# Causal attention on one Trainium2 core: scores, turned probabilities and values issued two items a period

## The chip, the cores and the metric

The kernel runs on one core of one Trainium2 chip. The metric is the device time of one execution in microseconds (us); three executions were timed. A difference is judged against what three executions of this kernel can tell apart.

## The reference

Two transformer blocks over 512 tokens of width 1024. The first block is a gated delta layer and then a sparse attention layer, each with an MLP. The part that matters here is the attention layer's two causal branches, "selected" and "window". With 512 tokens, 16 blocks chosen of 8 and a window of 512, both are plain causal softmax attention over 16 heads with 64 columns each, with their own keys and values and their own gate:

```
scale = dh ** -0.5
...
p_s = masked_softmax(jnp.einsum('bqghd,bgqkd->bghqk', qr, k_sel), (kpos <= t[:, None])[:, :, None])
o_s = jnp.einsum('bghqk,bgqkd->bqghd', p_s, v_sel)
...
p_w = masked_softmax(jnp.einsum('bqghd,bkgd->bghqk', qr, kwin), m_w)
o_w = jnp.einsum('bghqk,bkgd->bqghd', p_w, vwin)
g = take(gates)
o = g[..., 0:1] * o_c + g[..., 1:2] * o_s + g[..., 2:3] * o_w
```

The second block (latent attention beside a Fourier branch, two layers) is not touched.

## The kernel before, in words

All engines run fixed programs, in order, and wait for each other by semaphores. Weights stream through a ring of three blocks: a DMA brings `raw`, ScalarE rounds it to `w_hi` (L1724), GpSimd takes the rest as `w_lo` (L3480), TensorE does three matmuls for each product (L957 to L959). PSUM has eight banks; `plan_core` gives every product a bank and a count, `claim` waits until the bank's last reader has released it, `fill` announces it and `read` waits until it has been read.

The causal stage works through 48 items, `NSA_ITEMS`: for each of 8 pairs of heads (`j`) the six steps of `NSA_STEPS`. An item is one tile of 128 queries (`qt`) with one or both of the branches, for the two heads `s` = 0 and 1. Its width for a head is 2, 4, 3, 3, 4, 4 tiles of 128 keys for the steps 0 to 5; steps 0 and 1 hold both branches. The items of this text are written by their number n and step n mod 6. Each passes through six pieces of work:

- **S(n)**, TensorE, L1444 and L1448: scores into a pair of banks, (4, 5) for even n and (0, 1) for odd n. Three passes for two heads, on tiles of 64 rows, and four or eight small bf16 matmuls that add the causal mask.
- **max(n)**, VectorE, L3130: the row maxima. Then **exp(n)**, ScalarE, L2263: two or four exponentials with row sums into `prob[n % 4]`; with the last the scores' banks are free.
- **scale(n)**, VectorE, L3137 and L3142: reciprocals of the sums, and two or four multiplications of `prob` by reciprocal and gate.
- **T(n)**, TensorE, L1459: 2w transposes (w is the width) of `prob` into banks 6 and 7, one bank for each head.
- **copy(n)**, ScalarE, L2256: the turned probabilities out of both banks into `probT[n % 4]`, in one instruction.
- **V(n)**, TensorE, L1479: 4w matmuls of 128 columns, on tiles of 64 columns, adding to the output bank 2 or 3 of the head pair. At step 0 of each head pair from j = 2 on, four matmuls of `block_values` (L1433, "BV") stand ahead of V; those of j = 0 and 1 stand behind S(1).

When a head pair has its last V, ScalarE rounds the output (`a_hi`, L2271) and VectorE takes the rest (`a_lo`, L3121). ScalarE also rounds two weight blocks in the stage.

The order before, for i = 0 to 50, is S(i), T(i-2), V(i-3) on TensorE; copy(i-2), exp(i) on ScalarE; max(i), scale(i-1) on VectorE. Steady state is one item of each kind for each i.

Of the kernel before, what the change touches and what calls it, by code (L numbers as in the profile page):

```python
# [23 lines left out]
ACT = mybir.ActivationFunctionType  # L24
ALU = mybir.AluOpType
# [31 lines left out]
NSA_STEPS = [(0, (0, 1)), (1, (0, 1)), (2, (0,)), (2, (1,)), (3, (0,)), (3, (1,))]  # L57
NSA_ITEMS = [(j, qt, brs) for j in range(8) for qt, brs in NSA_STEPS]
NSA_LAST = len(NSA_STEPS) - 1


NSA_PARTS = [("q", 0), ("q", 1), ("keys", 0), ("keys", 1), ("q", 2), ("q", 3)]
# [313 lines left out]
def plan_core():  # L376
# [18 lines left out]
    def take_pair(key, b):  # L395

        take(key, b)
        beside[key] = uses[b + 1]
# [520 lines left out]
def prob_count(n, s, b):  # L919

    full, rest = divmod(n, len(NSA_STEPS))
    widths = [2 * len(brs) for _, brs in NSA_STEPS]
    return full * sum(widths) + sum(widths[:rest]) + s * len(NSA_ITEMS[n][2]) + b + 1


def program_tensor(pe, nc, c, block, bank, split, beside, early, sum_blocks):
# [23 lines left out]
    def read(key):  # L950

        b, n, _ = bank[key]
        pe.wait_ge(c.bank_read[b], n + 1)
# [472 lines left out]
    halves_of = [slice(64 * s, 64 * s + 64) for s in range(2)]  # L1426
    outs = {}

    def block_values(j):
# [5 lines left out]
    for i in range(len(NSA_ITEMS) + 3):  # L1435
        if i < len(NSA_ITEMS):
            j, qt, brs = NSA_ITEMS[i]
            end, out, both = (qt + 1) * P, claim_pair(("s1", i)), slice(brs[0], brs[-1] + 1)
            halves = [out[:, s, 0:len(brs) * end].rearrange("p (b k) -> p b k", b=len(brs)) for s in range(2)]
            if i % len(NSA_STEPS) == 0 and j in NSA_PARTS_FROM:  # L1440
                pe.wait_ge(c.score_lo, NSA_PARTS_FROM[j])
            for n, (q, k) in enumerate(((c.q_lo1, c.keys_hi), (c.q_hi1, c.keys_lo), (c.q_hi1, c.keys_hi))):
                for s, r in enumerate(halves_of):
                    mm(halves[s], q[r, j, qt * P:end], k[r, both, j // 4, 0:end], start=n == 0, stop=False)  # L1444
            for part, first in ((0, 64), (1, 0)):
                for s, r in enumerate(halves_of):
                    at = qt * P + 64 * part
                    ins = mm(halves[s][:, :, at:at + 64], c.causal16[r, first:first + P],  # L1448
                             c.causal16[r, 192:256].unsqueeze(1).to_broadcast([64, len(brs), 64]), start=False, stop=part == 1)
            ins.then_inc(fill(("s1", i)), 1)  # L1450
        if 2 <= i < len(NSA_ITEMS) + 2:
            n = i - 2
            j, qt, brs = NSA_ITEMS[n]
            out = claim_pair(("t1", n))
            for s in range(2):
                for b in range(len(brs)):
                    pe.wait_ge(c.prob_ready, prob_count(n, s, b))
                    for kt in range(b * (qt + 1), (b + 1) * (qt + 1)):
                        ins = nc.tensor.transpose(out[:, s, kt * P:kt * P + P], c.prob[:, n % 4, s, kt * P:kt * P + P], ident)  # L1459
            ins.then_inc(fill(("t1", n)), 1)  # L1460
        if i == 1:
# [6 lines left out]
        if i >= 3:  # L1468
            n = i - 3
            j, qt, brs = NSA_ITEMS[n]  # L1470
            if j > 1 and n % len(NSA_STEPS) == 0:
                block_values(j)
            read(("t1", n))
            last = n % len(NSA_STEPS) == NSA_LAST
            for b, br in enumerate(brs):
                for kt in range(qt + 1):
                    for s, o_rows in enumerate(halves_of):
                        v0, at = br * 256 + (2 * (j // 4) + s) * 64, (b * (qt + 1) + kt) * P
                        ins = mm(outs[j][o_rows, qt * P:qt * P + P], c.v[:, kt, v0:v0 + 64], c.probT[:, n % 4, s, at:at + P],  # L1479
                                 start=False, stop=last and kt == qt)  # L1480
            if last:
                ins.then_inc(c.attn_out, 1)
# [215 lines left out]
def program_scalar(act, nc, c, block, bank, split, beside, early, n_blocks, sums, squares_behind):  # L1698
# [73 lines left out]
    def release(key):  # L1772
        return c.bank_read[bank[key][0]]
# [477 lines left out]
    for i in range(len(NSA_ITEMS) + 3):  # L2251
        if 2 <= i < len(NSA_ITEMS) + 2:
            key, (_, qt, brs) = ("t1", i - 2), NSA_ITEMS[i - 2]
            n, end = i - 2, len(brs) * (qt + 1) * P
            filled(key)
            f(c.probT[:, n % 4, :, 0:end], c.pairs[bank[key][0] // 2][:, :, 0:end], ACT.Copy).then_inc(release(key), 1)  # L2256
        if i < len(NSA_ITEMS):
            key, (_, qt, brs), end = ("s1", i), NSA_ITEMS[i], (NSA_ITEMS[i][1] + 1) * P
            act.wait_ge(c.nb_ready, i + 1)
            for s in range(2):  # L2260
                for b in range(len(brs)):
                    e, m = slice(b * end, (b + 1) * end), s * len(brs) + b
                    ins = f(c.prob[:, i % 4, s, e], c.pairs[bank[key][0] // 2][:, s, e], ACT.Exp, bias=c.nb[:, i % 4, m:m + 1],  # L2263
                            accum_out=c.nb[:, i % 4, 4 + m:5 + m])
            ins.then_inc(release(key), 1)
        if i in (5, 11):
            weights(first + 4 + i // 6)
        if i >= 4 and (i - 4) % len(NSA_STEPS) == NSA_LAST:
            j = (i - 4) // len(NSA_STEPS)
# [246 lines left out]
def program_vector(dve, nc, c, block, bank, split, early, sums):  # L2516
# [25 lines left out]
    def step(ins):  # L2542

        ins.then_inc(c.vector_step, 1)
        count["step"] += 1
        dve.wait_ge(c.vector_step, count["step"])
# [577 lines left out]
    for i in range(len(NSA_ITEMS) + 2):  # L3124
        if i < len(NSA_ITEMS):
            key, (_, qt, brs) = ("s1", i), NSA_ITEMS[i]
            n, end = len(brs), (qt + 1) * P
            filled(key)
            scores = c.pairs[bank[key][0] // 2][:, :, 0:n * end].rearrange("p s (b k) -> p s b k", b=n)
            v.reduce_max(c.nb[:, i % 4, 0:2 * n].rearrange("p (s b) -> p s b", s=2), scores, axis=AX, negate=True)\  # L3130
                .then_inc(c.nb_ready, 1)
        if 1 <= i <= len(NSA_ITEMS):
            n = i - 1
            j, qt, brs = NSA_ITEMS[n]
            read(("s1", n))
            w, end = 2 * len(brs), (qt + 1) * P
            step(v.reciprocal(c.nb[:, n % 4, 8:8 + w], c.nb[:, n % 4, 4:4 + w]))  # L3137
            for s in range(2):
                for b, br in enumerate(brs):
                    m, g = 8 + s * len(brs) + b, NSA_H * (1 + br) + 2 * j + s  # L3140
                    e = c.prob[:, n % 4, s, b * end:(b + 1) * end]
                    v.tensor_scalar(e, e, c.nb[:, n % 4, m:m + 1], c.gate[:, qt, g:g + 1], ALU.mult, ALU.mult)\  # L3142
                        .then_inc(c.prob_ready, 1)
        if i >= 5 and (i - 5) % len(NSA_STEPS) == NSA_LAST:
            out_parts((i - 5) // len(NSA_STEPS))
    out_parts(7)
    sums_before_norm(3, "out", 1)

# [403 lines left out]
```

## Time and profile before

| | |
|---|---|
| median of three executions | 2000.17 us (2000.13 to 2001.76) |
| the profiled execution | 2002.18 us, of which the span of the profile 2000.1 us |
| causal stage in the span, first S to first matmul of the output projection | 767.18 to 903.53 us, 136.35 us |
| TensorE clock granted in the stage | full (1.00) |

A line of the profile gives the source line, the engine (PE is TensorE's matmuls, PEld its weight loads, DVE VectorE, ACT ScalarE), the operation, output and inputs by the program's names, and the shape. A matmul's end is modelled, so its stated length is longer than the step to the next one's start; the starts tell how fast TensorE goes on.

### The profile page before, as it was taken

How to read it: one execution, taken by the hardware profiler on the slowest of the kernel's cores; microseconds unless marked ns; L12 is line 12 of the kernel's file. 1: busy time of each engine (PE TensorE's matmuls, PEld its weight loads, DVE VectorE, ACT ScalarE, POOL GpSimd, SP SyncE). 2: the span in 40 equal slices, each digit the busy share in tenths (PEclk: the TensorE clock that was granted, in tenths of full speed). 3: DMA queues.
4: the chain of work that ended last, by engine and by line, in shares of the span. 5: the costliest groups of instructions: out<-in, count | busy, mean ns of one | idle time of the engine just before them, and what ended most of it. 6: DMA issues, size and time to landing. Idle time of an engine off the chain costs nothing.

```text
span 2000.1 us, 31685 instructions
## 1 busy us (share of the span) xinstructions
PE 1978.2 (99%) x12682; PEld 1662.3 (83%) x12682; DVE 1272.2 (64%) x2271; ACT 1056.8 (53%) x1770; POOL 749.2 (37%) x380
## 2 busy tenths in 40 slices
PE   8999999999999999999999999999999999999999
PEld 6877788988988887778888889878789987878897
DVE  7885556566656358873665665667777734777781
ACT  7752465444436327883643443567664544767441
POOL 3442134444444641003444444344044444413543
PEclk9999999999999999999999999999999999999999
DMA  4442123333322431002233333222013322211332
GB/s 163 127 133 83 48 87 106 104 103 100 106 96 95 142 106 38 12 2 99 95 106 99 104 104 103 87 95 85 23 53 106 105 96 95 77 40 42 102 103 93
DMA packets 62465, 178.18 MB, mean 89 GB/s; under 512 B 17760, under 2 KB 18144, under 8 KB 62320
## 3 DMA queue, kind: packets, MB, share of 16 engines
q1 hardware_dynamic: 47312, 166.99, 25.4%
q10 hardware_dynamic: 15008, 9.16, 1.7%
q8 instruction: 102, 1.67, 0.3%
q14 instruction: 43, 0.35, 0.1%
HBM read 170.85 MB, written 3.70 MB: 87 GB/s over the span
## 4 chain that ended last, share of the span: by engine, by line
PE 87%; DVE 7%; ACT 4%; issue 2%; POOL 0%; DMA 0%; ACTq 0%; DVEq 0%
PE banks L957 18%; PE banks L958 18%; PE banks L959 18%; PE banks L1075 6%; PE banks L1076 6%; PE banks L1077 6%; PE banks L1459 2%; PE banks L1479 2%; PE banks L1444 2%; PE banks L1555 1%; PE banks L1570 1%; PE banks L1583 1%; PE banks L1561 1%; ACT prob L2373 1%; PE banks L1356 1%
## 5 line engine op out<-in xcount | busy, mean ns | idle before, releaser
L3480 POOL TENSOR_TENSOR w_lo<-raw,w_hi 128x1024 fp32r<-128x1024 f32 (+4 forms) x348 | 714.0, 2058 | 1115.4 <-ACT w_hi L1724 962.4
L1724 ACT ACTIVATE w_hi<-raw 128x1024 fp32r<-128x1024 f32 (+2 forms) x272 | 261.8, 963 | 410.2 <-PE banks L959 285.7
L957 PE MATMUL banks<-h_lo,w_hi 128*128 128x512 f32 (+1 forms) x800 | 321.9, 402 | 10.1 <-POOL w_lo L3480 10.1
L957 PE MATMUL banks<-a_lo,w_hi 128*128 128x512 f32 x832 | 329.4, 396 | 0.0
L958 PE MATMUL banks<-a_hi,w_lo 128*128 128x512 f32 x832 | 324.6, 390 | 0.0
L959 PE MATMUL banks<-a_hi,w_hi 128*128 128x512 f32 x832 | 324.0, 389 | 0.0
L959 PE MATMUL banks<-h_hi,w_hi 128*128 128x512 f32 (+1 forms) x800 | 313.2, 392 | 0.0
L958 PE MATMUL banks<-h_hi,w_lo 128*128 128x512 f32 (+1 forms) x800 | 312.8, 391 | 0.0
L2613 DVE TENSOR_TENSOR x<-x,banks 128x512 f32<-128x512 f32 x168 | 115.3, 686 | 212.7 <-PE banks L959 212.7
L957 PEld LDWEIGHTS banks<-h_lo,w_hi 128*128 128x128 f32 (+1 forms) x800 | 150.2, 188 | 47.0 <-POOL w_lo L3480 8.2
L957 PEld LDWEIGHTS banks<-a_lo,w_hi 128*128 128x128 f32 x832 | 156.1, 188 | 39.4 <-DVE x L2613 7.4
L959 PEld LDWEIGHTS banks<-a_hi,w_hi 128*128 128x128 f32 x832 | 156.2, 188 | 33.4
L958 PEld LDWEIGHTS banks<-a_hi,w_lo 128*128 128x128 f32 x832 | 156.2, 188 | 31.1 <-issue 1.0
L959 PEld LDWEIGHTS banks<-h_hi,w_hi 128*128 128x128 f32 (+1 forms) x800 | 150.1, 188 | 33.1 <-issue 0.7
L958 PEld LDWEIGHTS banks<-h_hi,w_lo 128*128 128x128 f32 (+1 forms) x800 | 150.4, 188 | 32.4 <-issue 2.6
L2642 DVE TENSOR_TENSOR w_lo_s<-banks,w_hi_s 128x1024 fp32r<-128x1024 f32 x52 | 63.5, 1220 | 87.3 <-ACT w_hi_s L1753 87.3
L1075 PE MATMUL banks<-h_lo,w_hi 128*128 128x256 f32 x304 | 84.7, 279 | 1.8 <-POOL w_lo L3480 1.8
L1075 PE MATMUL banks<-t_lo,w_hi_s 128*128 128x256 f32 x312 | 86.1, 276 | 0.0
L1076 PE MATMUL banks<-t_hi,w_lo_s 128*128 128x256 f32 x312 | 86.1, 276 | 0.0
L1077 PE MATMUL banks<-t_hi,w_hi_s 128*128 128x256 f32 x312 | 86.1, 276 | 0.0
L1077 PE MATMUL banks<-h_hi,w_hi 128*128 128x256 f32 x304 | 84.5, 278 | 0.0
L1076 PE MATMUL banks<-h_hi,w_lo 128*128 128x256 f32 x304 | 84.4, 278 | 0.0
(500 smaller groups left out, 4166.6 us busy)
## 6 DMA issues: line engine op xcount, KB each, us to landing
raw<-in_weights SPq DMA_DIRECT2D x309, 512.0 KB, 3.3
x<-in_x SPq DMA_DIRECT2D x4, 512.0 KB, 5.7
AT<-row_dram ACTq DMA_DIRECT2D x4, 512.0 KB, 8.0
out<-x SPq DMA_DIRECT2D x8, 256.0 KB, 2.0
eg<-row_dram ACTq DMA_DIRECT2D x8, 128.0 KB, 3.9
phase<-in_phase ACTq DMA_DIRECT2D x1, 706.0 KB, 3.9
phase<-in_phase ACTq DMA_DIRECT2D x1, 640.0 KB, 3.8
ld_dram<-Ld ACTq DMA_DIRECT2D x2, 256.0 KB, 3.7
```

The source lines that it names most:

```text
L957: mm(out, w_hi, x_lo, start=first, stop=False, skip_group_check=shared)
L958: mm(out, w_lo, x_hi, start=False, stop=False, skip_group_check=shared)
L959: return mm(out, w_hi, x_hi, start=False, stop=last, skip_group_check=shared)
L1075: mm(out, w_hi, x_lo, start=half == k == n % 2 == 0, stop=False, skip_group_check=True)
L1076: mm(out, w_lo, x_hi, start=False, stop=False, skip_group_check=True)
L1077: ins = mm(out, w_hi, x_hi, start=False, stop=half == k == 1, skip_group_check=True)
L1444: mm(halves[s], q[r, j, qt * P:end], k[r, both, j // 4, 0:end], start=n == 0, stop=False)
L1459: ins = nc.tensor.transpose(out[:, s, kt * P:kt * P + P], c.prob[:, n % 4, s, kt * P:kt * P + P], ident)
L1724: ins = f(c.w_hi[:, b % RING, cols], c.raw[:, b % RING, cols], ACT.Copy)
L2613: tt_op(c.x[:, m, :], c.x[:, m, :], out[:, :], ALU.add).then_inc(release(key), 1)
L2642: tt_op(low, c.pairs[SUM_BANKS[0] // 2][:, :, :].rearrange("p b t -> p (b t)"), high.bitcast(F32), ALU.subtract)\
L3480: return nc.gpsimd.tensor_tensor(c.w_lo[:, slot, to], c.raw[:, slot, first:end], c.w_hi[:, slot, to].bitcast(F32), ALU.subtract)
```

## The change

TensorE takes the items in periods of two. Period k issues S(2k), T(2k-4), V(2k-6), V(2k-5), T(2k-3), S(2k+1). Periods 0 to 3 are the start (`early`), periods 24 to 26 the end. ScalarE's order in period k is exp(2k-1), copy(2k-4), exp(2k), copy(2k-3); VectorE's is max(2k-1), scale(2k-2), max(2k), scale(2k-1). The turned probabilities of the two heads have keys of their own, so that each of the banks 6 and 7 is claimed, filled, copied by an instruction of its own and released by itself. An exponential now also waits for T(n-4), whose `prob` it overwrites. The output's `a_hi` and `a_lo` and the two weight blocks get places in the periods. VectorE's instructions are the same ones in the same order, but for the places of `a_lo`.

```diff
+def causal_period(k):
+    early = [([], [], []), ([0], [], []), ([1], [0], []), ([2], [1], [3])]
+    lists = early[k] if k < len(early) else ([2 * k - 4], [2 * k - 6, 2 * k - 5], [2 * k - 3])
+    return [[n for n in items if n < len(NSA_ITEMS)] for items in lists]
+
+CAUSAL_PERIODS = len(NSA_ITEMS) // 2 + 3
...
-        take_pair(("t1", n), 6)
+        for s in range(2):
+            take(("t1", n, s), 6 + s)
...
+    def turned1(n):
+        j, qt, brs = NSA_ITEMS[n]
+        for s in range(2):
+            out = claim(("t1", n, s))
+            for b in range(len(brs)):
+                pe.wait_ge(c.prob_ready, prob_count(n, s, b))
+                for kt in range(b * (qt + 1), (b + 1) * (qt + 1)):
+                    ins = nc.tensor.transpose(out[:, kt * P:kt * P + P], c.prob[:, n % 4, s, kt * P:kt * P + P], ident)
+            ins.then_inc(fill(("t1", n, s)), 1)
...
+    for k in range(CAUSAL_PERIODS):
+        first_turned, valued, then_turned = causal_period(k)
+        if 2 * k < len(NSA_ITEMS):
+            scores1(2 * k)
+        for n in first_turned:
+            turned1(n)
+        for n in valued:
+            values1(n)
+        for n in then_turned:
+            turned1(n)
+        if 2 * k < len(NSA_ITEMS):
+            scores1(2 * k + 1)
...
+    def exponentials(i):
+        key, (_, qt, brs), end = ("s1", i), NSA_ITEMS[i], (NSA_ITEMS[i][1] + 1) * P
+        if i >= 4:
             for s in range(2):
+                filled(("t1", i - 4, s))
+        act.wait_ge(c.nb_ready, i + 1)
...
+    def turned_back_1(n):
+        _, qt, brs = NSA_ITEMS[n]
+        end = len(brs) * (qt + 1) * P
+        for s in range(2):
+            key = ("t1", n, s)
+            f(c.probT[:, n % 4, s, 0:end], filled(key)[:, 0:end], ACT.Copy).then_inc(release(key), 1)
+
+    for k in range(CAUSAL_PERIODS):
+        first_turned, _, then_turned = causal_period(k)
+        if 0 <= 2 * k - 1 < len(NSA_ITEMS):
+            exponentials(2 * k - 1)
+        for n in first_turned:
+            turned_back_1(n)
+        if 2 * k < len(NSA_ITEMS):
+            exponentials(2 * k)
+        for n in then_turned:
+            turned_back_1(n)
+        if k in (3, 6):
+            weights(first + 3 + k // 3)
+        if k >= 5 and (k - 5) % 3 == 0 and (k - 5) // 3 < 7:
...
+    for k in range(CAUSAL_PERIODS):
+        if k and 2 * k - 1 < len(NSA_ITEMS):
+            maxima(2 * k - 1)
+            scaled_probs(2 * k - 2)
+        if 2 * k < len(NSA_ITEMS):
+            maxima(2 * k)
+        if k and 2 * k - 1 < len(NSA_ITEMS):
+            scaled_probs(2 * k - 1)
+        if k >= 6 and (k - 6) % 3 == 0:
+            out_parts((k - 6) // 3)
```

## Rows read from the trace of the kernel before

**Rows 1.** The page: busy time, share of the span and instructions of the engines.
```profile
PE 1978.2 (99%) x12682; PEld 1662.3 (83%) x12682; DVE 1272.2 (64%) x2271; ACT 1056.8 (53%) x1770; POOL 749.2 (37%) x380
```

**Rows 2.** Busy time by stretch: stage, and one head pair (window, length, PE, PEld, DVE, ACT).
```profile
767.18:903.53 136.35, 134.09 (x1473) 97.68 (x1472) 109.86 (x234) 113.07 (x315) 4.90 (x2) 1.00 0.03 9
806.63:823.41 16.78, 16.78 (x186) 12.23 (x184) 13.63 (x30) 13.83 (x39) 0.00 (x0) 1.00 0.01 2
```

**Rows 3.** The chain in order of time, stage's middle (start, us to next piece, what).
```profile
836.13 0.72 PE banks L1444 x6
...
836.93 0.59 PE banks L1459 x4
...
840.36 1.00 PE banks L1433 x4
...
846.52 0.81 PE banks L1479 x12
...
848.00 1.02 PE banks L1459 x8
...
849.83 0.90 PE banks L1444 x6
...
850.85 1.02 PE banks L1459 x8
```

**Rows 4.** Timeline, TensorE inside one S group and into the T behind it.
```profile
825.10 0.50 PE L1444 MATMUL banks<-keys_hi,q_lo 64*128 64x512 f32 x2
825.44 0.39 PE L1444 MATMUL banks<-keys_lo,q_hi 64*128 64x512 f32 x2
...
825.91 0.23 PE L1448 MATMUL banks<-causal 64*128 64x64 bf16 x4
826.07 0.88 PE L1459 MATMUL banks<-common,prob 128*128 128x128 f32 x6
```

**Rows 5.** Timeline, TensorE in the second block's attention, which has V before T.
```profile
1418.75 1.09 PE L1583 MATMUL banks<-probT,v 128*64 128x128 f32 x16
1419.78 1.09 PE L1570 MATMUL banks<-common,prob 128*128 128x128 f32 x8
...
1422.40 0.39 PE L1555 MATMUL banks<-k_hi,q_hi 64*128 64x512 f32 x2
1422.63 0.48 PE L1555 MATMUL banks<-k_hi,q_r 64*128 64x512 f32 x2
```

**Rows 6.** ScalarE's and VectorE's groups by shape, the stage (count, busy, mean ns).
```profile
L2256 ACT ACTIVATE probT<-banks 128x1024 f32<-128x1024 f32 x24 | 24.6, 1026 | 11.4 <-PE banks L1459 11.4
L2263 ACT ACTIVATE prob<-banks,nb 128x512 f32<-128x512 f32 x32 | 21.7, 689 | 0.0
```

**Rows 7.** Timeline: exponentials and copy of step 1; half copies; VectorE's maxima.
```profile
786.73 0.47 ACT L2263 ACTIVATE prob<-banks,nb 128x256 f32<-128x256 f32 x1
...
788.53 0.62 ACT L2256 ACTIVATE probT<-banks 128x512 f32<-128x512 f32 x1
...
826.18 1.23 DVE L3130 TENSOR_REDUCE nb<-banks 128x2 f32<-128x1024 f32 x1 [1.50 <-PE banks L1448]
...
1414.98 0.60 ACT L2381 ACTIVATE probT<-banks 128x512 f32<-128x512 f32 x1
1415.46 0.61 ACT L2383 ACTIVATE probT<-banks 128x512 f32<-128x512 f32 x1
```

**Rows 8.** Timeline, the stage's start and end.
```profile
773.13 0.45 PE L1444 MATMUL banks<-keys_hi,q_lo 64*128 64x384 f32 x2 [0.39 <-ACT prob L2263]
...
773.93 1.05 PEld L1459 LDWEIGHTS banks<-common,prob 128*128 128x128 f32 x8
...
774.46 0.24 ACT L2263 ACTIVATION_READ_ACCUMULATOR prob<-banks,nb 128x1 f32 x1
...
898.09 0.86 PEld L1459 LDWEIGHTS banks<-common,prob 128*128 128x128 f32 x8 [0.67 <-ACT probT L2256]
...
900.30 0.86 PEld L1459 LDWEIGHTS banks<-common,prob 128*128 128x128 f32 x8 [0.55 <-ACT probT L2256]
```

More of the change, by code:

```diff
@@ L1427, in program_tensor, with scores1 @@
     outs = {}
+    def scores1(i):
+        j, qt, brs = NSA_ITEMS[i]
+        end, out, both = (qt + 1) * P, claim_pair(("s1", i)), slice(brs[0], brs[-1] + 1)
+        halves = [out[:, s, 0:len(brs) * end].rearrange("p (b k) -> p b k", b=len(brs)) for s in range(2)]
+        if i % len(NSA_STEPS) == 0 and j in NSA_PARTS_FROM:
+            pe.wait_ge(c.score_lo, NSA_PARTS_FROM[j])
+        for n, (q, k) in enumerate(((c.q_lo1, c.keys_hi), (c.q_hi1, c.keys_lo), (c.q_hi1, c.keys_hi))):
+            for s, r in enumerate(halves_of):
+                mm(halves[s], q[r, j, qt * P:end], k[r, both, j // 4, 0:end], start=n == 0, stop=False)
+        for part, first in ((0, 64), (1, 0)):
+            for s, r in enumerate(halves_of):
+                at = qt * P + 64 * part
+                ins = mm(halves[s][:, :, at:at + 64], c.causal16[r, first:first + P],
+                         c.causal16[r, 192:256].unsqueeze(1).to_broadcast([64, len(brs), 64]), start=False, stop=part == 1)
+        ins.then_inc(fill(("s1", i)), 1)
+    def turned1(n):
[7 more added lines that the diff above has]
+            ins.then_inc(fill(("t1", n, s)), 1)
     def block_values(j):
@@ L1433, in block_values @@
             mm(outs[j][o_rows, :], c.vcb[r, 2 * (j // 4) + s, :], c.pcT[r, j // 2, :], start=True, stop=False)
[L1435 to L1461, printed above, removed]
@@ new lines, in values1 @@
+    def values1(n):
+        j, qt, brs = NSA_ITEMS[n]
+        if j > 1 and n % len(NSA_STEPS) == 0:
+            block_values(j)
+        for s in range(2):
+            read(("t1", n, s))
+        last = n % len(NSA_STEPS) == NSA_LAST
+        for b, br in enumerate(brs):
+            for kt in range(qt + 1):
+                for s, o_rows in enumerate(halves_of):
+                    v0, at = br * 256 + (2 * (j // 4) + s) * 64, (b * (qt + 1) + kt) * P
+                    ins = mm(outs[j][o_rows, qt * P:qt * P + P], c.v[:, kt, v0:v0 + 64], c.probT[:, n % 4, s, at:at + P],
+                             start=False, stop=last and kt == qt)
+        if last:
+            ins.then_inc(c.attn_out, 1)
@@ L1467, in program_tensor @@
             block_values(1)
[L1468 to L1482, printed above, removed]
     for m in range(KT):
@@ L2250, in program_scalar @@
         f(c.v[:, tt, :], c.psum[bank[("v", tt)][0]][:, :], ACT.Copy, scale=c.tiny[:, 20 + tt:21 + tt]).then_inc(release(("v", tt)), 1)
[L2251 to L2259, printed above, removed]
-            for s in range(2):
[L2261 to L2269, printed above, removed]
@@ new lines, in exponentials @@
+    def exponentials(i):
+        key, (_, qt, brs), end = ("s1", i), NSA_ITEMS[i], (NSA_ITEMS[i][1] + 1) * P
+        if i >= 4:
+            for s in range(2):
+                filled(("t1", i - 4, s))
+        act.wait_ge(c.nb_ready, i + 1)
+        for s in range(2):
+            for b in range(len(brs)):
+                e, m = slice(b * end, (b + 1) * end), s * len(brs) + b
+                ins = f(c.prob[:, i % 4, s, e], c.pairs[bank[key][0] // 2][:, s, e], ACT.Exp, bias=c.nb[:, i % 4, m:m + 1],
+                        accum_out=c.nb[:, i % 4, 4 + m:5 + m])
+        ins.then_inc(release(key), 1)
@@ new lines, in turned_back_1 @@
+    def turned_back_1(n):
+        _, qt, brs = NSA_ITEMS[n]
+        end = len(brs) * (qt + 1) * P
+        for s in range(2):
+            key = ("t1", n, s)
[13 more added lines that the diff above has]
+        if k >= 5 and (k - 5) % 3 == 0 and (k - 5) // 3 < 7:
+            j = (k - 5) // 3
@@ L3122, in out_parts @@
             .then_inc(release(("o1", j)), 1)
[L3124 to L3145, printed above, removed]
@@ new lines, in maxima, with scaled_probs @@
+    def maxima(i):
+        key, (_, qt, brs) = ("s1", i), NSA_ITEMS[i]
+        n, end = len(brs), (qt + 1) * P
+        filled(key)
+        scores = c.pairs[bank[key][0] // 2][:, :, 0:n * end].rearrange("p s (b k) -> p s b k", b=n)
+        v.reduce_max(c.nb[:, i % 4, 0:2 * n].rearrange("p (s b) -> p s b", s=2), scores, axis=AX, negate=True)\
+            .then_inc(c.nb_ready, 1)
+    def scaled_probs(n):
+        j, qt, brs = NSA_ITEMS[n]
+        w, end = 2 * len(brs), (qt + 1) * P
+        read(("s1", n))
+        step(v.reciprocal(c.nb[:, n % 4, 8:8 + w], c.nb[:, n % 4, 4:4 + w]))
+        for s in range(2):
+            for b, br in enumerate(brs):
+                m, g = 8 + s * len(brs) + b, NSA_H * (1 + br) + 2 * j + s
+                e = c.prob[:, n % 4, s, b * end:(b + 1) * end]
+                v.tensor_scalar(e, e, c.nb[:, n % 4, m:m + 1], c.gate[:, qt, g:g + 1], ALU.mult, ALU.mult).then_inc(c.prob_ready, 1)
```

1 line of the change is left out of this document (added).

## The prediction, made before the changed kernel was run

> **What bounds the kernel now.** I read the page first: TensorE is busy for 99% of the span, VectorE for 64% and ScalarE for 53% [rows 1]. Then the stretch of the changed stage: it takes 136.35 us, and one head pair of six items takes 16.78 us, in which TensorE never rests, while VectorE is busy for 13.63 and ScalarE for 13.83 us [rows 2]. So in steady state only TensorE's time counts, and the others have some 3 us to spare in each head pair; what can spoil that is the order of their work, not its amount.
>
> Then the chain in order of time, for what TensorE does in those 16.78 us. The groups have a pattern. Four transposes take 0.59 us, eight take 1.02; twelve value matmuls take 0.81 and sixteen 1.03 [rows 3, 5]. So a transpose costs (1.02 - 0.59) / 4 = 0.107 us, a value matmul half of that, and each group has a fixed part of 0.59 - 0.43 = 0.165 us, whatever its size. The other way round (values, then transposes) it is the same: sixteen value matmuls take 1.03 to the next transpose, 16 x 0.054 + 0.165 [rows 5]. A scores group has a fixed part too: the first pass takes 0.34 where a pass between like passes takes 0.23, so 0.11 at the start; and the four mask matmuls take 0.16 before the transposes start, though they stream only 2 x 64 columns, so about 0.1 at the end [rows 4, 5]. Of 16.78 us, some 3 are such changes of kind.
>
> Last the two ends of the stage, where the pipeline fills and drains: of 136.35 us, 8 x 16.78 = 134.2, less 1.0 since the first two BV run together, leaves 3.1 us of waits, all at the two ends [rows 2, 8]. (The two BV are four matmuls each, 1.00 us [rows 3].)
>
> **The change, part by part.** *Pairs on TensorE.* Before, two items have six changes of kind (S to T to V, twice). After, S(2k+1) stands before S(2k+2) and V(2k-6) before V(2k-5), which leaves four. New value pairs: 22 (the last, V(46) and V(47), stood together before). New score pairs: 22. What a pair saves is not shown directly for values. Bounds: nothing, if a met wait in front of the second group costs as much as a change of kind; the whole 0.165, if it costs nothing. For scores, the second block's attention has two such groups in a row, and the first pass of the second starts 0.23 after the last pass of the first, the plain step, though a wait stands there [rows 5]. That is nearest, so I take 0.165 for values, and for scores, between 0.11 (start only) and 0.21 (both ends), 0.165. Sum: 22 x 0.165 + 22 x 0.165 = -3.6 - 3.6 = -7.2 us.
>
> The Trainium skill bears on this: "TensorEngine Tiling (Array Packing)", Key Properties, says that a change of tiling mode drains TensorE. Scores run on 64-row tiles, masks too, values on 64-column tiles, transposes on the whole array, so by that rule both ends of a score pair are saved, the sum of the pairs would be 22 x 0.165 + 22 x 0.21 = -8.3 us, and a second group of one kind is free.
>
> *The two banks by themselves.* The copy of 128x1024 took 1.03 us [rows 6]; two of 128x512 in the second block take 0.48 between starts and 0.61 for the last, 1.09 together [rows 7]. So each item adds some 0.07 us to ScalarE, 0.4 a head pair, to 14.3 of the about 16.5 available: hidden, by ScalarE's spare time, as long as nothing queued behind it is late. In return bank 6 is free after the first half.
>
> *The order on ScalarE.* Here is what is late next. In period k ScalarE does exp(2k-1) before copy(2k-4). But S(2k-1) is TensorE's last group of period k-1, and T(2k-3) needs the banks that copy(2k-4) empties. Queued behind exp(2k-1) on ScalarE are so copy(2k-4), and behind that, on TensorE, T(2k-3), then all scores. Take the periods with k = 4, 7, ... 22, where 2k-1 is step 1 with four wide exponentials, and count from where S(2k-1) makes way:
> - the other engines: 0.11 until VectorE's maximum starts [rows 4, 7], 1.23 the maximum, 1.80 the four exponentials (786.73 to 788.53), 0.60 the first half of the copy [rows 7], and 0.08 for two hand-overs (an estimate, each under the 0.11 seen): 3.82 us.
> - TensorE: S(2k) 0.80, less 0.165 for the pair; T(2k-4), eight transposes, 1.02; V(2k-6) and V(2k-5), twelve matmuls each, 0.81 + 0.81 - 0.165 [rows 3]: 3.11 us.
> So T(2k-3) waits 0.71 us for bank 6, and about 0.05 more for bank 7: 0.75 us, seven times, +5.3 us. Before, copy(i-2) stood ahead of exp(i), and no such wait shows in the steady part.
>
> The other periods have room. Where 2k-1 is step 3, two exponentials of 384 replace four, about 2.7 against 3.3 us. Where it is step 5, the exponentials take 2 x 0.69 less overlap [rows 6] and the chain about 3.25 us, against 3.75 us of TensorE with the BV, 1.00 [rows 3]. Only head pair 1 has no BV at that place: once +0.5 us. The next wait in line, S(2k+2) on exp(2k), has chains of 4.7 to 4.8 us against 5 us or more. The waits of exp(n) on T(n-4) are met long before.
>
> *The start.* S(4) now comes straight after S(3), at 773.13 + 0.80 - 0.165 = 773.77, and needs exp(2), which ends at 774.70 [rows 8], plus 0.1 for the split copy of item 0 ahead of it: it waits 1.0 us. S(6) comes after V(0) and S(5) (8 x 0.054 + 0.165 = 0.6, and 0.97 from 825.10 to 826.07 [rows 4], less 0.165: 1.4 us) behind T(1), while ScalarE does copy(1), 1.1, and exp(4), 1.4, behind T(1): it waits about 1.2 us. T(1), whose eight weight loads took 1.05 us instead of 0.86 [rows 8] for waits on VectorE, no longer waits (0.2). Together +2.0 us.
>
> *The end.* T(46) waits for a copy before, its weight loads idle for 0.67 us, 0.5 more than the 0.17 of a plain change of kind; T(47) waits 0.4 (0.55 less 0.17) [rows 8]. After, T(46) still waits for copy(45), while T(47) comes after V(44) and V(45) and V(47) after V(46), so their waits go, 0.4 and about 0.1: -0.5 us.
>
> VectorE's work is unchanged, its order too; the moved weight roundings and `a_hi` have whole periods of slack.
>
> Sum: -7.2 + 5.3 + 0.5 + 2.0 - 0.5 = +0.1, so with the roundings 0 to 0.5 us; I take +0.3. The sum is made against the profiled execution, 2002.18 us with a span of 2000.1; the median of the three executions is 2000.17, 2.0 below that execution. All that follows the stage is bound by TensorE and moves along. Forecast: 2000.17 + 0.3 = 2000.5 us.
>
> **The rivals.**
> - *Paid back (forecast).* Pairs save, the wait at T(2k-3) eats it. For it: both rows are there, with 0.7 us between the two chains. 2000.5 us, own range 1998 to 2003.
> - *Faster.* The wait doesn't appear, as the copy comes before TensorE gets there. That takes 3.82 us to shrink to 3.11; against it, that every piece of the chain is measured. Price: -7.2 + 2.0 - 0.5 = -5.7, so 1994.5 us.
> - *Slower: a pair saves nothing*, since the second group's weights aren't loaded before its wait is met. It decides from a boundary cost of about 0.15 us inside a pair on. Then TensorE's path is 3.44 us, the wait 0.4 us, seven times 3.0; the start and the end add 2.2 - 0.5, head pair 1 0.3: +5.0, so 2005.2 us. For it: no row shows values behind values; against it the 0.23 of [rows 5].
>
> **How the numbers follow.** Paid back 0.68, faster 0.14, pairs that save nothing or another such wait on S(2k+2) 0.18. 0.2% is 4.0 us: faster than 1996.2 is the second case, slower than 2004.2 the third. That 0.2% is also about what a measurement of this kernel can tell from no change. The range takes in the bounds of the pair (0 to 0.21) and of the chain (3.82 give or take 0.2, seven times, 1.4 us): 1995.3 to 2005.0.
>
> **What would show it.** In the changed profile: S to S and V to V with no gap of weight loads; the stage's head pair at 16.5 to 16.6 us instead of 16.78; in one of three periods TensorE waiting 0.7 us before transposes, put down to ScalarE's copy (L2256's successor); waits of about 1 us on exponentials before S(4) and S(6); stage length 136 to 137 us. The prediction is wrong if the head pair takes 15.9 us (no wait), or 17 and more (a second wait, or pairs without gain).

## The result, and the profile of the changed kernel

The changed kernel takes 2004.13 us (median of 18 executions, 2003.21 to 2005.05), the kernel before 1999.58 us (18 executions in turn with them, 1998.84 to 2001.76). The ratio is 1.0021, 95% interval 1.0015 to 1.0028: 4.5 us slower, just past the 0.2% that the prediction named as its bound (the interval reaches to both sides of it). Forecast were 2000.5 us, no change. The time lies inside the predicted range (1995.3 to 2005.0), but outside the 1998 to 2003 of the case called likeliest, and only 0.1 us under the 2004.2 from which the slower case was to begin.

The profiled execution of the changed kernel took 2004.22 us (span 2002.3). That of the kernel before, 2002.18 us, stood 2.6 us above its own median, and its stage began 1.75 us later than this one's (767.18 against 765.43), though nothing ahead of the stage was changed. Most of that is TensorE's clock. Far ahead of the stage, behind a wait of 2.24 us, that execution has a short stretch at half clock (window, length, PE, PEld, DVE, ACT, POOL, granted clock, DMA):

```profile
118.00:120.00 2.00, 2.00 (x6) 1.52 (x6) 1.86 (x5) 1.15 (x2) 2.00 (x1) 0.50 0.12 49
```

There the starts of ten matmuls of 512 columns, from 116.62 to 120.26, lie 3.64 us apart in all, where nine plain steps of 0.227 make 2.04: 1.6 us lost. So the comparison goes by the length of the stage and not by the spans. The page, and the windows of stage and head pair (window, length, PE, PEld, DVE, ACT, POOL, granted clock, DMA):

```profile
PE 1972.7 (99%) x12682; PEld 1661.2 (83%) x12682; DVE 1272.9 (64%) x2271; ACT 1058.9 (53%) x1818; POOL 748.3 (37%) x380
```

```profile
765.43:906.03 140.60, 129.50 (x1473) 97.02 (x1472) 111.97 (x234) 115.47 (x363) 4.79 (x2) 1.00 0.03 9
825.09:841.88 16.79, 16.07 (x187) 12.08 (x188) 13.37 (x30) 14.06 (x46) 0.00 (x0) 1.00 0.00 1
```

Against [rows 2]: the stage is 4.25 us longer (140.60 against 136.35), while TensorE is busy in it for 4.6 us less (129.50 against 134.09). So TensorE needs less time for its work, as the pairs should give, and its idle time grew by more, from 2.3 to 11.1 us. A head pair of the steady part is as long as before (16.79 against 16.78) with 0.7 us of idle time in it. Eight head pairs like this one give no loss; the 4.25 us were lost elsewhere, and the timeline finds them near the stage's start. Behind the stage both kernels take the same: 2002.3 - 906.03 = 1096.3 us, and before 2000.1 - 903.53 = 1096.6.

The waits of the stage (who waited, for whom, us in total, times, the longest):

```profile
PEld banks L1464 <- ACT probT L2295: 8.1, 11, 1.0
PEld banks L1449 <- ACT prob L2286: 6.2, 6, 1.4
PE banks L1464 <- ACT probT L2295: 5.6, 9, 0.7
PE banks L1449 <- ACT prob L2286: 4.5, 5, 1.2
```

Transposes (L1464) wait for the copy (L2295) nine times, 5.6 us; scores (L1449) wait for the exponentials (L2286) five times, 4.5 us. Of the five, the one before S(2), 0.48 us, has its like in the kernel before (0.18 before S(2), 0.39 before S(3)); the other four are new. The timeline of one period of the steady part, k = 10:

```profile
834.37 0.29 PE L1453 MATMUL banks<-causal 64*128 64x128 bf16 x4
...
834.47 0.42 PE L1449 MATMUL banks<-keys_hi,q_lo 64*128 64x384 f32 x2
...
834.70 1.23 DVE L3170 TENSOR_REDUCE nb<-banks 128x4 f32<-128x1024 f32 x1 [1.04 <-PE banks L1453]
...
835.25 1.09 PE L1464 MATMUL banks<-common,prob 128*128 128x128 f32 x8
...
836.04 0.47 ACT L2286 ACTIVATE prob<-banks,nb 128x256 f32<-128x256 f32 x1 [1.31 <-DVE nb L3170]
836.05 1.12 DVE L3182 TENSOR_SCALAR prob<-prob,nb,gate 128x128 f32<-128x128 f32 x4
...
836.27 1.53 PE L1484 MATMUL banks<-probT,v 128*64 128x128 f32 x24
...
837.86 1.09 ACT L2295 ACTIVATE probT<-banks 128x512 f32<-128x512 f32 x2
...
838.51 1.14 PE L1464 MATMUL banks<-common,prob 128*128 128x128 f32 x8 [0.71 <-ACT probT L2295]
...
839.59 0.44 PE L1449 MATMUL banks<-keys_hi,q_lo 64*128 64x384 f32 x2
```

This is the wait that was forecast. Count from the start of S(2k) at 834.47: TensorE needs 0.78 for the scores, 1.02 for the transposes and 24 x 0.054 + 0.165 = 1.46 for the two V, which ends at 837.73. The other engines need 4.04: the maximum from 834.70, the exponentials from 836.04, the copy from 837.86, and the transposes start at 838.51. TensorE loses 0.78 us, and 0.06 more inside the group (1.08 from 838.51 to 839.59, where 1.02 is the undisturbed time).

The waits that were not forecast stand near the stage's start. Timeline, where ScalarE rounds a block of weights (L1749) and GpSimd takes the rest (L3528):

```profile
782.35 1.22 DVE L3170 TENSOR_REDUCE nb<-banks 128x4 f32<-128x1024 f32 x1 [1.17 <-PE banks L1453]
...
782.67 1.12 ACT L1749 ACTIVATE w_hi<-raw 128x1024 fp32r<-128x1024 f32 x1
...
783.70 3.15 DVE L3182 TENSOR_SCALAR prob<-prob,nb,gate 128x128 f32<-128x128 f32 x4
...
783.86 2.39 POOL L3528 TENSOR_TENSOR w_lo<-raw,w_hi 128x1024 fp32r<-128x1024 f32 x1 [24.84 <-ACT w_hi L1749]
...
789.12 0.50 PE L1449 MATMUL banks<-keys_hi,q_lo 64*128 64x512 f32 x2 [1.02 <-ACT prob L2286]
```

VectorE's four multiplications of item 6 take 3.15 us; four of the same shape took 1.12 us at 836.05. In that time GpSimd's subtraction ran. It is one of the four that is long: it took 2.38 us from 783.96 on, to 0.09 us behind the end of the subtraction (783.86 + 2.39 = 786.25), and the three others took 0.33 to 0.34 us each. The next maximum came late, with it the exponentials, and the scores of item 10 waited 1.02 us. The same happens at item 12: four multiplications from 801.25 take 3.16, GpSimd runs from 801.42 for 2.40, and S(16) waits 1.03 at 806.67. In the kernel before, the same subtraction fell elsewhere:

```profile
783.62 2.45 POOL L3480 TENSOR_TENSOR w_lo<-raw,w_hi 128x1024 fp32r<-128x1024 f32 x1 [23.14 <-ACT w_hi L1724]
...
784.79 1.22 DVE L3130 TENSOR_REDUCE nb<-banks 128x4 f32<-128x1024 f32 x1 [0.96 <-PE banks L1448]
...
786.14 1.12 DVE L3142 TENSOR_SCALAR prob<-prob,nb,gate 128x128 f32<-128x128 f32 x4
```

It lay beside VectorE's wait and its maximum, which kept its usual 1.22 us; the multiplications began as it had ended (783.62 + 2.45 = 786.07).

### The profile page after: what moved, and what is told of

It reads as the page before. It is cut to its first block, busy times and chain, and to the rows that moved or that the text cites. A ratio compares the mean times of both kernels' runs of the same rounds, so it can differ in the third digit from the quotient of the medians.

```text
span 2002.3 us, 31873 instructions
## 1 busy us (share of the span) xinstructions
PE 1972.7 (99%) x12682; PEld 1661.2 (83%) x12682; DVE 1272.9 (64%) x2271; ACT 1058.9 (53%) x1818; POOL 748.3 (37%) x380
## 4 chain that ended last, share of the span: by engine, by line
PE 88%; DVE 6%; ACT 4%; issue 1%; POOL 0%; ACTq 0%; DMA 0%; DVEq 0%
PE banks L969 19%; PE banks L970 19%; PE banks L971 19%; PE banks L1087 6%; PE banks L1088 6%; PE banks L1089 6%; PE banks L1464 2%; PE banks L1484 1%; PE banks L1449 1%; PE banks L1580 1%; PE banks L1595 1%; ACT prob L2286 1%; PE banks L1608 1%; PE banks L1033 1%; DVE nb L3170 1%
## 5 line engine op out<-in xcount | busy, mean ns | idle before, releaser
L3528 POOL TENSOR_TENSOR w_lo<-raw,w_hi 128x1024 fp32r<-128x1024 f32 (+4 forms) x348 | 713.1, 2055 | 1118.4 <-ACT w_hi L1749 965.1
L1749 ACT ACTIVATE w_hi<-raw 128x1024 fp32r<-128x1024 f32 (+2 forms) x272 | 261.9, 963 | 407.2 <-PE banks L971 280.3
```

Of the source, the lines that this page charges most:

```text
L1749: ins = f(c.w_hi[:, b % RING, cols], c.raw[:, b % RING, cols], ACT.Copy)
L3528: return nc.gpsimd.tensor_tensor(c.w_lo[:, slot, to], c.raw[:, slot, first:end], c.w_hi[:, slot, to].bitcast(F32), ALU.subtract)
```

## The experiments

Two theories stood at the beginning. **Collision**: of the 4.25 us, 2.5 to 3 come from VectorE's multiplications that stand still while GpSimd subtracts; without that the forecast balance holds. **Rival**: the pairs and the waits explain it by themselves, that is, the long multiplications are covered, and the loss comes from the new order on ScalarE and TensorE or from the split copies. The first four kernels ran beside one kernel before (median 1999.72 us, 33 executions), the last three beside another series of it (1999.34 us, 27 executions). Intervals are at 95%. The stage's length in the one profiled execution is the second measure.

**1. The subtraction cut short.** The changed kernel, with GpSimd's part of the two stage blocks taken over 128 columns and not 1024:

```diff
+                if b - block[("v", 0)][0] in (4, 5):
+                    n = P
                 if end < n:
                     ins = low_part(b % RING, end, n, 0)
```

> The changed kernel, but GpSimd's subtraction for the two weight blocks of the stage covers 128 of their 1024 columns; the rest of those low parts is left out, so the output isn't the reference's. Theory 1 (VectorE's multiplications of items 6 and 12 took 3.15 us instead of 1.12 because they ran into the 2.40 us subtraction, and TensorE waited behind them): both fall back to about 1.1 to 1.4 us, the wait of TensorE before S(10) and S(16) goes, and the kernel is 2.5 to 3 us faster than the changed one, 1.5 to 2 us (0.1%) slower than before. Rival (the multiplications were slow for their place, by ScalarE or by PSUM, and TensorE's waits come from the order alone): they stay at 3 us, and the time stays at 4.5 us over before.

Measured: 2001.83 us, ratio 1.0010 (1.0001 to 1.0019). The stage, and item 6:

```profile
764.54:902.69 138.15, 129.15 (x1473) 96.89 (x1472) 108.35 (x234) 115.39 (x363) 0.97 (x2) 1.00 0.03 9
```

```profile
782.75 1.26 DVE L3182 TENSOR_SCALAR prob<-prob,nb,gate 128x128 f32<-128x128 f32 x4
...
782.93 0.49 POOL L3528 TENSOR_TENSOR w_lo<-raw,w_hi 128x128 fp32r<-128x128 f32 x1 [24.85 <-ACT w_hi L1749]
```

With a subtraction of 0.49 us the multiplications take 1.26 instead of 3.15, and the stage is 140.60 - 138.15 = 2.45 us shorter. The two waits before S(10) and S(16) are gone; the forecast waits before transposes (0.72) remain. That is at the lower end of the 2.5 to 3 us expected; the medians give 2.3 (2004.13 to 2001.83, from two series).

**2. The subtraction moved.** The changed kernel with all its work, the two roundings one period later:

```diff
-        if k in (3, 6):
-            weights(first + 3 + k // 3)
+        if k in (4, 7):
+            weights(first + 3 + (k - 1) // 3)
```

> The changed kernel, all of its work, but the two weight blocks are rounded one period later (k = 4 and 7 instead of 3 and 6), behind the two copies of a period in which ScalarE is not in front of a step-1 item. Theory 1: what counts is only where the 2.40 us subtraction falls against VectorE's multiplications; there it falls beside those of step 2 and 3, on the least loaded stretch, so some 3 us come back, 138.2 us for the stage instead of 140.6, the kernel 1.5 to 2.5 us over before. Rival: no difference from the changed kernel (within 0.7 us), since the same work is queued on ScalarE.

Measured: 2001.61 us, ratio 1.0011 (1.0001 to 1.0020).

```profile
765.62:903.52 137.90, 129.24 (x1473) 97.00 (x1473) 109.02 (x233) 115.33 (x363) 5.17 (x2) 1.00 0.03 9
```

The stage is 2.70 us shorter than the changed kernel's, with the same work. But 0.31 of that was there before the first rounding: S(6) starts 12.13 us behind the stage's start here and 12.44 there (12.38 in experiment 1). So both experiments give some 2.4 us for the collision. The multiplications of item 6 take 1.12 again. GpSimd now runs at 789.60 for 2.59 us, beside the two wider ones of item 9, which take 1.59 instead of 0.87 us; no wait of TensorE follows from it. So what a collision costs depends on the multiplications it meets and on what is queued behind them.

**3. The copy ahead of the exponentials.** Experiment 2, and in the periods with the wait the copy goes first:

```diff
+        copy_first = k >= 4 and k % 3 == 1
+        if copy_first:
+            for n in first_turned:
+                turned_back_1(n)
         if 0 <= 2 * k - 1 < len(NSA_ITEMS):
             exponentials(2 * k - 1)
-        for n in first_turned:
-            turned_back_1(n)
+        if not copy_first:
+            for n in first_turned:
+                turned_back_1(n)
```

> As the run with the later rounding, and in the periods k = 4, 7, ... 22 ScalarE does copy(2k-4) before exp(2k-1), so that T(2k-3) finds its bank free. Theory of the prediction (the copy queued behind four exponentials costs 0.7 us seven times): the wait before these T goes entirely, but exp(2k-1) and exp(2k) now end 1.3 us later, so about 0.6 of the 0.75 us comes back as waits of S(2k+1) and S(2k+2) on exponentials: 1.0 to 1.5 us faster than the run with the later rounding, the kernel level with before to 1 us over. Rival (the bank wait alone is what costs, ScalarE has slack): the whole 5 us come back, the kernel is 3 us faster than before.

Measured: 1999.94 us, ratio 1.0002 (0.9993 to 1.0011): level with the kernel before, and 1.7 us under experiment 2 (1.0 to 1.5 were expected), though the two intervals overlap. Head pair and, as it stands out, the granted clock near the stage's start (window, length, PE, PEld, DVE, ACT, POOL, clock):

```profile
829.05:845.61 16.56, 16.23 (x187) 12.18 (x185) 13.30 (x31) 14.06 (x46) 0.00 (x0) 1.00 0.01 2
772.00:774.00 2.00, 1.22 (x6) 0.63 (x6) 1.96 (x6) 1.13 (x5) 0.00 (x0) 0.77 0.00 0
774.00:776.00 2.00, 2.00 (x14) 1.75 (x12) 1.96 (x5) 1.40 (x5) 0.00 (x0) 0.50 0.04 8
776.00:778.00 2.00, 1.93 (x20) 1.14 (x18) 0.68 (x3) 1.74 (x5) 0.00 (x0) 0.88 0.00 0
```

```profile
834.03 1.53 PE L1484 MATMUL banks<-probT,v 128*64 128x128 f32 x24
...
835.49 1.09 PE L1464 MATMUL banks<-common,prob 128*128 128x128 f32 x8
...
836.66 0.44 PE L1449 MATMUL banks<-keys_hi,q_lo 64*128 64x384 f32 x2
...
837.29 0.23 PE L1453 MATMUL banks<-causal 64*128 64x64 bf16 x4
...
837.78 0.50 PE L1449 MATMUL banks<-keys_hi,q_lo 64*128 64x512 f32 x2 [0.26 <-ACT prob L2286]
```

The wait before the transposes is gone: they follow the V at 835.49, 834.03 + 1.46. But the exponentials come later, and the scores wait for them: those at 836.66 stand 0.15 behind 835.49 + 1.02, and those at 837.78 come 0.49 behind the last mask group at 837.29, where 0.07 is the step inside a pair (840.21 to 840.28 in the changed kernel). That is 0.15 + 0.42 = 0.57 of the 0.84 given back, and the head pair is 0.23 shorter. So the cause of the wait is ScalarE's order, shown, and each order makes something late: within these periods the chain from scores to the freed bank is too long for the distance that TensorE leaves. The stage of this execution, 137.81 us, holds stretches at a clock below full and is not used for sizes. That the copy's place is the cause is shown by the wait that goes; that the chain is too long for any order is argued from these two orders alone.

**4. The split copies alone.** The kernel before, with a key, a bank and a copy for each head and everything else as it was:

```diff
-        take_pair(("t1", n), 6)
+        for s in range(2):
+            take(("t1", n, s), 6 + s)
...
-            filled(key)
-            f(c.probT[:, n % 4, :, 0:end], c.pairs[bank[key][0] // 2][:, :, 0:end], ACT.Copy).then_inc(release(key), 1)
+            for s in range(2):
+                key = ("t1", n, s)
+                f(c.probT[:, n % 4, s, 0:end], filled(key)[:, 0:end], ACT.Copy).then_inc(release(key), 1)
```

> The kernel before with one part of the change alone: each turned bank claimed, filled and copied by itself, the order of everything as before. Theory (the split costs ScalarE 0.07 us an item, which its spare time hides): steady state 16.78 us a head pair, the waits of T(46), T(47) and V(47) shorter by some 0.6 us together, the time within 1 us of before. Rival (48 more instructions on ScalarE cost at their full price): 3 us slower.

Measured: 1998.52 us, ratio 0.9996 (0.9987 to 1.0004).

```profile
765.45:901.45 136.00, 133.92 (x1474) 97.68 (x1473) 109.17 (x234) 116.03 (x363) 5.18 (x2) 1.00 0.03 9
806.00:822.78 16.78, 16.78 (x186) 12.23 (x184) 13.47 (x30) 14.21 (x47) 0.00 (x0) 1.00 0.01 1
```

ScalarE is busy for 0.38 us more in a head pair (14.21 against 13.83), the head pair is as long as before, 16.78, and the stage 0.35 shorter: T(47) no longer waits, T(46) waits as before (0.46). The split costs nothing and is no part of the loss.

**5. Other pairs.** If the pairs save and the loss is in the order, then an order that leaves the exponentials more distance should keep the gain. Period k now issues S(2k), T(2k-3), S(2k+1), T(2k-2), V(2k-4), V(2k-3): only the V are paired, the scores stand apart. ScalarE's order stays exp(2k-1), copy(2k-3), exp(2k), copy(2k-2); the roundings stand at k = 4 and 7, and `a_hi` and `a_lo` a period earlier than in the change.

```diff
-    early = [([], [], []), ([0], [], []), ([1], [0], []), ([2], [1], [3])]
-    lists = early[k] if k < len(early) else ([2 * k - 4], [2 * k - 6, 2 * k - 5], [2 * k - 3])
+    lists = ([2 * k - 3], [2 * k - 4, 2 * k - 3], [2 * k - 2])
...
-        for n in valued:
-            values1(n)
-        for n in then_turned:
-            turned1(n)
         if 2 * k < len(NSA_ITEMS):
             scores1(2 * k + 1)
+        for n in then_turned:
+            turned1(n)
+        for n in valued:
+            values1(n)
```

> Pairs of values alone: period k is S(2k), T(2k-3), S(2k+1), T(2k-2), V(2k-4), V(2k-3) on TensorE, and exp(2k-1), copy(2k-3), exp(2k), copy(2k-2) on ScalarE; the banks are split as in the change, the two weight blocks rounded in periods 4 and 7. Theory (a pair of values saves 0.146 us as the changed kernel's trace shows, a T whose copy has a whole S group in front of the next T never waits, and a lag of 2 to 3 items costs the start nothing more than before): 16.34 us a head pair instead of 16.78, no waits of T in the steady part, the stage 133.4 us instead of 136.35, the kernel 2.5 to 3.5 us (0.15%) faster than before. Rival (any second item in a period costs a wait of its own, so pairs cannot pay): the waits come back at T(2k-2) or at S, and the time is level with before or slower.

Measured: 1996.56 us, ratio 0.9985 (0.9977 to 0.9994): 2.8 us faster than the kernel before, and the fastest of all.

```profile
764.47:897.29 132.82, 130.03 (x1473) 98.23 (x1472) 107.69 (x234) 115.47 (x363) 4.74 (x2) 1.00 0.03 10
822.96:839.29 16.33, 16.33 (x185) 12.30 (x185) 13.39 (x30) 14.05 (x46) 0.00 (x0) 1.00 0.01 2
```

```profile
833.04 0.66 PE L1463 MATMUL banks<-common,prob 128*128 128x128 f32 x4
833.63 1.97 PE L1483 MATMUL banks<-probT,v 128*64 128x128 f32 x32
835.52 0.50 PE L1448 MATMUL banks<-keys_hi,q_lo 64*128 64x512 f32 x2
```

In a head pair TensorE never rests, and it is 16.78 - 16.33 = 0.45 us shorter, three value pairs of 0.15 each. The 32 value matmuls take 1.89 us to the next group, and 32 x 0.054 + 0.165 = 1.89: the second V has no fixed part that shows. Eight head pairs would give 3.6 us, and the stage is 136.35 - 132.82 = 3.5 us shorter. So pairs of values are worth nearly what was forecast, once nothing waits. Several things were changed at once here (no score pairs, other distances, the roundings in their later places), so the experiment shows that value pairs pay, and not which of these took the waits away.

**6. The collision put into the kernel before.** Nothing but the place of the roundings changes, from behind exp(5) and exp(11) to behind exp(6) and exp(12):

```diff
-        if i in (5, 11):
-            weights(first + 4 + i // 6)
+        if i in (6, 12):
+            weights(first + 3 + i // 6)
```

> The kernel before with its two weight roundings one item later (after exp(6) and exp(12) instead of exp(5) and exp(11)), nothing else. Theory 1 (VectorE's multiplications stand still while GpSimd subtracts): scale(6) and scale(12) take about 3 us instead of 1.12, TensorE waits about 1.5 us behind each, the kernel is 2.5 to 3.5 us slower than before. Rival (it was the order of the pairs, the roundings' place doesn't matter): no difference.

Measured: 2003.10 us, ratio 1.0017 (1.0008 to 1.0026).

```profile
764.38:904.13 139.75, 135.16 (x1474) 97.93 (x1473) 114.06 (x234) 113.17 (x315) 4.72 (x2) 1.00 0.03 9
```

```profile
783.64 3.21 DVE L3142 TENSOR_SCALAR prob<-prob,nb,gate 128x128 f32<-128x128 f32 x4
...
783.90 2.36 POOL L3480 TENSOR_TENSOR w_lo<-raw,w_hi 128x1024 fp32r<-128x1024 f32 x1 [25.88 <-ACT w_hi L1724]
...
786.39 0.84 PE L1459 MATMUL banks<-common,prob 128*128 128x128 f32 x3 [1.04 <-DVE prob L3142]
...
787.17 1.09 PE L1479 MATMUL banks<-probT,v 128*64 128x128 f32 x16
```

Two roundings moved by one item each lengthen the stage by 3.40 us (139.75 against 136.35) and the kernel by 3.8, a little more than the 2.5 to 3.5 expected. The multiplications of item 6 take 3.21 with GpSimd's 2.36 inside, and TensorE waits for VectorE directly, in the middle of the four transposes of item 6: its idle time is 1.04 us, here and at item 12. From the first transpose, at 785.02, to the V behind them at 787.17 pass 2.15 us, where four transposes take 0.59 [rows 3]; at item 12 it is 2.14 (802.35 to 804.49). That makes 3.1 of the 3.40 us. The kernel before only escaped this by where its roundings happened to fall.

**7. The collision put into experiment 5?** Its roundings one period earlier, at k = 3 and 6, the places of the changed kernel:

```diff
-        if k in (4, 7):
-            weights(first + 3 + (k - 1) // 3)
+        if k in (3, 6):
+            weights(first + 3 + k // 3)
```

> As the run with pairs of values alone, but the two weight blocks rounded in periods 3 and 6, as in the change. Theory 1 (the place of the subtraction against VectorE's multiplications decides): one of the multiplications' groups is stretched each time and the kernel is about 1 us slower than the run with roundings in periods 4 and 7, still 1.5 to 2.5 us faster than before. Rival: equal to it within 0.3 us.

Measured: 1997.13 us, ratio 0.9988 (0.9979 to 0.9997).

```profile
765.72:899.54 133.82, 130.15 (x1473) 98.25 (x1472) 108.29 (x234) 115.26 (x363) 4.73 (x2) 1.00 0.03 10
```

```profile
783.01 1.10 ACT L1748 ACTIVATE w_hi<-raw 128x1024 fp32r<-128x1024 f32 x1
...
784.20 2.37 POOL L3527 TENSOR_TENSOR w_lo<-raw,w_hi 128x1024 fp32r<-128x1024 f32 x1 [25.23 <-ACT w_hi L1748]
...
784.58 0.96 DVE L3169 TENSOR_REDUCE nb<-banks 128x2 f32<-128x768 f32 x1 [0.83 <-PE banks L1452]
...
786.00 0.44 PE L1448 MATMUL banks<-keys_hi,q_lo 64*128 64x384 f32 x2 [0.44 <-ACT prob L2285]
```

The stage is 1.00 us longer than in experiment 5, the medians differ by 0.6, which their intervals don't tell apart. And the reason is not the one I had in mind. The subtraction fell beside a maximum and not beside the multiplications of item 6, and the four of item 7 that it met at its end took 1.50 instead of 1.38. What costs is the rounding on ScalarE itself: its 1.10 us stand ahead of the exponentials of item 7, and scores wait 0.44 for them, here and at 801.82. So a rounding has two prices, its own place in ScalarE's queue and the place that it gives GpSimd.

## Why the prediction was right in part, and the step that failed

The terms of the sum, and what the trace of the changed kernel shows (us, + is slower):

| step | forecast | measured | by |
|---|---|---|---|
| 22 value pairs | -3.6 | -3.4 | 0.15 to 0.17 saved a pair |
| 22 score pairs | -3.6 | -2.6 | 0.11 to 0.14 saved a pair |
| T(2k-3) waits, seven times | +5.3 | +5.9 | 0.84 each |
| T(9) waits, once | +0.5 | +0.5 | 0.43 idle |
| the start | +2.0 | +2.1 | S(4), S(6) |
| the end | -0.5 | -0.9 | T(46) 0.2 less late, T(47) not late, V(46) and V(47) in 1.92, not 2.20 |
| split copies | 0 | 0 | experiment 4 |
| roundings | 0 to 0.5 | +2.5 | experiments 1 and 2 |
| sum | +0.1 (+0.3 taken) | +4.1 | stage +4.25, medians +4.5 |

**The step that failed** is the last term of the sum, 0 to 0.5 us for the roundings, and the sentence that it stands on: "VectorE's work is unchanged, its order too; the moved weight roundings and `a_hi` have whole periods of slack." The roundings have slack as to when their weights are needed. But a rounding moved on ScalarE moves GpSimd's subtraction too, and that decides which VectorE instruction it lies beside. The prediction never asked which. VectorE had the same instructions in the same order, and yet eight of them took 4.1 us longer (3.15 + 3.16 - 2 x 1.12). Experiments 1 and 2 remove the collision in two ways and shorten the stage by 2.45 and 2.70; experiment 6 makes one in the kernel before and loses 3.4. The rival that named the loss elsewhere (pairs that save nothing, or a second wait in the steady part) got the sign and not the cause: with the roundings out of the way (experiments 1 and 2) the changed kernel is 1.9 to 2.1 us slower than the one before, within the 0.2% that the forecast called no change. Their stages are 1.80 and 1.55 us longer, and the other rows of the table leave 4.1 - 2.5 = 1.6.

**What was luck.** The range took in errors of the pairs and of the chain, and none of a collision; that 2004.13 still lies in it is due to room that was meant for something else. It also left out the times of both rivals, 1994.5 and 2005.2 us, which had been given a chance of 0.32 together. And without the roundings' 2.5 the sum would have been off by 1.5 us all the same: score pairs that gave 1.0 less and waits that cost 0.6 more, with the end 0.4 better. The mechanism called likeliest, that the pairs save and the wait at T(2k-3) pays most of it back, did come about; the sign given for it, a stage of 136 to 137 us, did not (140.60).

The Trainium skill has the rule that I didn't bring to bear: "SBUF — State Buffer", Who interferes with whom, says that VectorE and GpSimd share one pair of ports as an exclusive lock held for a whole instruction, that a `tensor_scalar` can need it, and that a `tensor_reduce` on trn2 never does. The trace agrees with both: 3.15 instead of 1.12 for the multiplications, nearly all of it in the one that stood still for 2.38, and 1.22 unchanged for the maximum beside a subtraction of 2.45. The maximum here reads PSUM; no run has a reduction that reads SBUF beside GpSimd.

**Right, the value pair.** From the end of the stage:

```profile
892.20 1.97 PE L1484 MATMUL banks<-probT,v 128*64 128x128 f32 x32
894.09 1.09 PE L1464 MATMUL banks<-common,prob 128*128 128x128 f32 x8
```

Two V of sixteen matmuls take 1.89, against 2 x 1.03 [rows 5]; two of twelve take 1.46 (831.29 to 832.75), against 2 x 0.81 [rows 3]. That saves 0.17 and 0.16, and experiment 5 gives 0.15 a pair; 0.165 was taken.

**Mis-sized, the score pair**: 0.165 taken, 0.11 to 0.14 measured. The four masks take 0.10 before a score group instead of 0.22 before transposes (834.37 to 834.47, and 829.26 to 829.48), or 0.07 instead of 0.16 (840.21 to 840.28, and 841.07 to 841.23), and the first pass of the second group saves 0.02 only (0.32 against 0.34), not the 0.11 that the second block's row [rows 5] seemed to show. With this a head pair comes out as measured: 16.78 less three value pairs of 0.155 and three score pairs of 0.12, and 0.84 more for the wait, is 16.79. The bound of 0.21, both ends of a group, was further off still. The Trainium skill's rule in "TensorEngine Tiling (Array Packing)", Key Properties, is that a change of tiling mode drains TensorE; read as the prediction read it, with nothing left to pay inside a pair, it agrees with the value pairs, and the score pairs save only a part. No run had score pairs alone.

**Mis-sized, the wait at T(2k-3)**: place, number and releaser were right. The chain is 4.04 against 3.26 on TensorE, 0.78 apart where 0.71 was forecast (3.82 against 3.11). Both sides were put too short. On the chain the maximum starts 0.23 us after S(2k) has begun (834.47 to 834.70) and not 0.11, ScalarE starts 0.11 after the maximum has ended (834.70 + 1.23 to 836.04), where the two hand-overs together had been put at 0.08, and the first half of the copy takes 0.65 to TensorE's start. On TensorE S(2k) takes 0.78 and not 0.635, as the score pair saves less. Experiment 3 shows the cause.

**Right, the start**, by the trace and not by a run of its own:

```profile
773.10 0.50 PE L1449 MATMUL banks<-keys_hi,q_lo 64*128 64x512 f32 x2 [0.81 <-ACT prob L2286]
...
777.87 0.39 PE L1449 MATMUL banks<-keys_hi,q_lo 64*128 64x256 f32 x2 [1.16 <-ACT prob L2286]
```

S(4) and S(6) wait for exponentials, forecast 1.0 and 1.2. Behind the last mask group before each, S(4) comes 1.05 us (772.05 to 773.10) and S(6) 1.39 (776.48 to 777.87), where 0.07 is the step inside a pair: 0.98 and 1.32.

**Right, the split copies** (experiment 4, 0.38 us more of ScalarE in a head pair, forecast 0.4, hidden). **Half right, the head pair**: 16.5 to 16.6 us forecast and 16.79 measured, since the score pairs save less and the wait is longer.

**Mis-sized, the end**: in the kernel before, the steps in front of T(46) and T(47) were 1.33 and 1.18 us instead of 0.81, and V(46) and V(47) took 2.20 (901.33 to 903.53); in the changed kernel the step in front of T(46) is 1.12, T(47) comes on time, and the two V take 1.92. That is 0.9 us, where 0.5 was forecast.

What stays open: the measured terms come to 4.1, the one profiled stage to 4.25 and the medians to 4.5. Why a score pair keeps some 0.09 us of its 0.21 is not settled.

## What to carry to other kernels

An instruction of GpSimd that is "off the path" has a place in time all the same: when an edit moves it, or moves what it waits for, look up which VectorE instruction it will lie beside, and keep it beside idle time or, as far as these traces show it, beside reductions from PSUM. Grouping like work on TensorE pays its 0.15 us a pair only if the chain from the first product to the freed bank still fits; here pairing the values alone (2.8 us faster) was worth more than pairing everything (4.5 us slower, some 2.0 with the roundings out of the way). The likely reason, argued and not tested by itself, is that paired scores shorten the distance behind which the exponentials hide. Where an engine's order makes one thing late, swapping two steps of it makes the other late (0.84 us became 0.57); change the distance on the engine that waits.

## What was unexpected of the hardware

- VectorE's four multiplications of 128x128 took 3.15 to 3.21 us instead of 1.12 with a GpSimd subtraction of 2.36 to 2.40 inside: longer by 2.0 to 2.1, nearly the subtraction's length, and not by a share of it. One of the four took nearly all of it, 2.38 us instead of 0.34. GpSimd lost nothing there (2.39 against 2.45 beside a maximum); where it started in the middle of two wider multiplications (experiment 2, 789.60) it took 2.59. With the subtraction cut to 0.49 us they took 1.26.
- In two of the nine profiled executions TensorE's granted clock fell (the last 2 us of the span left aside). In that of experiment 3 it stood at 0.77, 0.50 and 0.88 in three stretches of 2 us from 772.00 on, 0.50 being the level of 1.2 GHz. TensorE was busy for 1.22 of the 2 us in which it fell, after a wait of 0.81 us. Eight transposes, at 774.29, took 1.97 us there instead of 1.09. The scores, the transposes and the V from 772.78 on took 1.5 us more than in the changed kernel, and 0.6 of it came back, as the wait before S(6) was 0.34 instead of the 0.90 of experiment 2. The changed kernel has the same wait of 0.81 us, and TensorE was busy for 1.19 us in the same stretch, but its clock read 1.00 there. The other is the profile of the kernel before, 0.50 at 118.00 to 120.00, behind a wait of 2.24 us that ended at 115.62; there it cost 1.6 us ahead of the stage. The other eight have waits of 1.3 to 1.7 us at that place, and their clock read 1.00 there. So what makes it fall is not settled; the wait of 0.81 us before S(4) came once with a fall and, in the changed kernel and experiments 1 and 2, three times without.
